# Three up-projections as seven half-size products each, and the last projection's first unit in another order

## The reference

```python
def hybrid_layer(x, mem, g_in, w_in, b_merge, g_mem, w_mem_kv, w_up_moba, w_up_dsa, w_up_cross, w_out):
    h = rmsnorm_2(x, g_in)
    z = h @ w_in          # split into (mq, mk, mv, mg, dq, dk, dv, dg, iq, ik, iw, xq, xg, glog)
    ...
    ya = moba_attention(mq, mk, heads(mv, MOBA_HEADS, HEAD_DIM)).reshape(B, S, MOBA_W)
    ya = (ya * jax.nn.silu(mg)) @ w_up_moba
    ...
    yb = (yb * jax.nn.silu(dg)) @ w_up_dsa
    ...
    yc = (yc * jax.nn.silu(xg)) @ w_up_cross
    gates = jax.nn.sigmoid(glog + b_merge).reshape(B, S, N_BRANCH_2, D_MODEL)
    u = gates[:, :, 0] * ya + gates[:, :, 1] * yb + gates[:, :, 2] * yc
    return x + u @ w_out
```

## Time and profile before

| what | value |
| --- | --- |
| median of 3 runs | 1574.53 us (1574.34 to 1576.32) |
| profiled execution, its own time | 1572.25 us |
| its span | 1570.5 us |
| mean granted TensorE clock over the span | 0.884 |
| from the end of `gl5` to the start of `w21` | 1494.80 to 1550.99 us |

### The profile page before, as it was taken

How to read it: one execution, slowest core, us unless ns; L and a number is a source line. 1 busy time by engine, 2 the same in 40 slices (tenths; PEclk the granted TensorE clock), 3 DMA queues, 4 the chain that set the end, 5 groups by cost and what they waited for, 6 DMA issues and landing times.

```text
span 1570.5 us, 21027 instructions
## 1 busy us (share of the span) xinstructions
PE 1257.4 (80%) x9222; PEld 818.6 (52%) x9222; DVE 562.7 (36%) x997; ACT 208.0 (13%) x426; POOL 2.8 (0%) x7
## 2 busy tenths in 40 slices
PE   9999999998666766665665665665666999999998
PEld 8989979974323312211221221221221588999986
DVE  5777467951001010010010010010010497798534
ACT  2003232020000000000000000000000211135401
POOL 0000000000000000000000000000000000000000
PEclk9999999999978977777777777787788999999999
DMA  9343274689999999999999999999999654434340
GB/s 374 143 162 139 85 264 170 271 362 433 443 428 433 437 431 433 434 434 436 434 432 434 436 434 432 434 437 434 431 431 430 275 214 161 161 109 170 112 153 36
DMA packets 20568, 506.61 MB, mean 323 GB/s; under 512 B 4240, under 2 KB 4368, under 8 KB 6544
## 3 DMA queue, kind: packets, MB, share of 16 engines
q1 hardware_dynamic: 20208, 505.28, 77.1%
q10 hardware_dynamic: 288, 0.26, 0.0%
HBM read 504.48 MB, written 1.05 MB: 322 GB/s over the span
## 4 chain that ended last, share of the span: by engine, by line
PE 54%; DMA 40%; DVE 4%; issue 1%; ACT 0%; SPq 0%; DVEq 0%; ACTq 0%
DMA ring<-in_experts 37%; PE psP L1400 13%; PE psP L779 10%; PE psP L1398 9%; PE psP L1347 8%; PE psP L827 4%; PE psA L842 2%; DMA arena<-in_experts 2%; DVE arena L2071 2%; PE psP L1440 2%; PE psB L1762 1%; PE psB L1333 1%; DVE ring L2071 1%; PE psA L758 1%; DMA X<-in_x 1%
## 5 line engine op out<-in xcount | busy, mean ns | idle before, releaser
L2071 DVE TENSOR_TENSOR X<-X,psA 128x512 f32<-128x512 f32 x66 | 45.2, 687 | 696.7 <-PE psA L842 682.5
L779 PE MATMUL psP<-ring,arena 128*32 128x512 f32 x1024 | 147.9, 730 | 127.8 <-DMA ring<-in_experts 127.8
L779 PE MATMUL psP<-arena 128*32 128x512 f32 x1024 | 145.3, 718 | 125.6 <-DMA arena<-in_experts 125.4
L779 PEld LDWEIGHTS psP<-ring,arena 128*32 128x32 f32 x1024 | 37.8, 131 | 234.4 <-issue 229.5
L779 PEld LDWEIGHTS psP<-arena 128*32 128x32 f32 x1024 | 35.0, 129 | 230.7 <-DMA arena<-in_experts 118.6
L1400 PE MATMUL psP<-arena,ring 128*128 128x128 f32 x992 | 116.9, 276 | 1.8 <-DVE score L2071 1.8
L1400 PEld LDWEIGHTS psP<-arena,ring 128*128 128x128 f32 x992 | 113.7, 192 | 3.0 <-issue 2.7
L827 PE MATMUL psP<-arena 128*32 128x512 f32 x512 | 73.8, 741 | 22.4 <-DMA arena<-in_experts 21.0
L827 PE MATMUL psP<-ring,arena 128*32 128x512 f32 x512 | 72.8, 726 | 23.3 <-DMA ring<-in_experts 21.9
L1400 PE MATMUL psP<-spare,ring 128*128 128x128 f32 x640 | 74.7, 275 | 0.0
L2071 DVE TENSOR_TENSOR ring<-ring 128x1024 f32<-128x1024 f32 x61 | 73.7, 1220 | 1.1 <-DMA ring<-in_u_dq 0.5
(11 more groups left out here) (354 smaller groups left out, 1429.7 us busy)
## 6 DMA issues: line engine op xcount, KB each, us to landing
arena<-in_experts SPq DMA_DIRECT2D x7, 4096.0 KB, 22.3
ring<-in_experts SPq DMA_DIRECT2D x7, 4096.0 KB, 23.3
ring<-in_u_gl SPq DMA_DIRECT2D x6, 2048.0 KB, 8.4
ring<-in_u_hq SPq DMA_DIRECT2D x2, 2048.0 KB, 22.6
ring<-in_u_hv SPq DMA_DIRECT2D x2, 2048.0 KB, 12.0
ring<-in_u_hg SPq DMA_DIRECT2D x2, 2048.0 KB, 8.6
ring<-in_u_ga SPq DMA_DIRECT2D x2, 2048.0 KB, 8.6
ring<-in_u_gb SPq DMA_DIRECT2D x2, 2048.0 KB, 9.0
```

Of the source, the lines that this page charges most:

```text
L779: mm = pe.matmul(z[j * CAP:(j + 1) * CAP, :], x[:, 4 * half + k, j * CAP:(j + 1) * CAP], held[c % 4][:, k // 2, j, (k % 2) * 512:(k % 2 + ...
L2071: return dve.tensor_tensor(o, a, b, op)
```

## The change

Each up-projection becomes seven products of half size in all three dimensions. `seven_up` issues them in two steps, four products and three, each product into a bank of its own (512 columns: 4 blocks of 128 outputs, 2 k, 128 tokens). Each step now uses both P0 and P1. `merge_up` adds up and gates each quarter at once. `halves` and `sums` get the three units; weight sums and half sums lie in areas of SBUF of their own. The end of the plan is written out anew, with sums and halves between the attention steps. `w20` gets an order of products of its own (`seven_final`), in which each product waits for the parts of the gated sum that it needs (`y_parts`), and `add_final` adds it up.

```diff
+OUT_PRODUCTS_2 = [(1, 0, 0), (2, 0, 256), (5, 0, 512), (6, 0, 768), (7, 1, 0), (3, 1, 256), (4, 1, 512)]
+UP_PRODUCTS = [[(2, 0, 0), (1, 0, 512), (6, 1, 0), (5, 1, 512)], [(7, 0, 0), (3, 0, 512), (4, 1, 0)]]
...
-    turn(9, 10, "gl5")
-    turn(10, None, "um0", "um1")
-    proj("ud0", "ud1")
-    sums("w20")
-    proj("ux0")
-    p.append(("halves_a", "z", ""))
-    proj("ux1")
+
+    p.append(("scores", 10, "A"))
+    sums("um")
+    p.extend([("halves", "um", ""), ("halves", "ud", ""), ("soft", 10, "")])
+    p.extend([("probsT", 9, "B"), ("normal", 10, ""), ("sums", ("ud", 0), "")])
+    p.extend([("head", ("gl5", 40), ""), ("pv", 9, "B")])
+    proj("gl5")
+    p.extend([("probsT", 10, "B"), ("sums", ("ud", 1), "")])
+    proj("um0")
+    p.append(("sums", ("ux", 0), ""))
+    proj("um1")
+    p.extend([("pv", 10, "B"), ("halves", "ux", ""), ("sums", ("ux", 1), "")])
+    proj("ud0")
+    p.append(("sums", ("w20", 0), ""))
+    proj("ud1")
+    p.append(("sums", ("w20", 1), ""))
+    proj("ux0", "ux1")
     p.append(("halves", "z", ""))
     proj("w20")
...
+            def seven_up(key, arg):
+
+                unit, step = arg[:2], int(arg[2])
+                regions, w, s = list(USE[key]), unit_ap(unit), h_sums[unit]
+                h = sg[{"m": "mg", "d": "dg", "x": "xg"}[unit[1]]]
+                t1, t2, t4 = sums_of(unit)
+                low, high = slice(0, 512), slice(512, 1024)
...
+                for n, half, at in UP_PRODUCTS[step]:
+                    (a, b), z = factors[n], ps[regions[half]]
+                    if n == 2:
+                        wait_empty(pe, ("pv", {"m": 8, "d": 5, "x": 10}[unit[1]]))
+                    if at == 0:
+                        may_fill(pe, key, regions[half])
+                    if n == 6:
+                        pe.wait_ge(halved, 4 * HALVES.index(unit) + 4)
+                        pe.wait_ge(summed, SUMMED[unit])
+                    if n == 4:
+                        pe.wait_ge(summed, SUMMED_LAST[unit])
+                    for o in range(4):
+                        for k in range(2):
+                            mm = pe.matmul(z[:, at + o * P:at + o * P + P], b[:, k, o * P:o * P + P], a[:, k, :],
+                                           start=(k == 0), stop=(k == 1))
...
+            def seven_final(key, arg):
...
+                for n, half, at in OUT_PRODUCTS_2:
+                    (a, b), z = factors[n], ps[regions[half]]
+                    if at == 0:
+                        may_fill(pe, key, regions[half])
+                    if n in (1, 2):
+
+                        pe.wait_ge(y_parts, {1: 1, 2: 3}[n])
+                    if n == 5:
+                        pe.wait_ge(summed, SUMMED_LAST[arg])
+                    if n in (5, 6, 7, 3):
+                        pe.wait_ge(halved, 4 * HALVES.index("z") + {5: 1, 6: 2, 7: 3, 3: 4}[n])
...
+            def merge_up(arg, key):
...
+                def gate(rows, t, n):
...
+                    y, x = gl[0][:, part, here], gl[g][:, part, here]
+                    if g == 0:
+                        i = tt(y, rows, y, ALU.mult)
+                    else:
+                        link(tt(x, rows, x, ALU.mult))
+                        i = tt(y, y, x, ALU.add)
+                    if g == 2:
+                        i.then_inc(y_parts, 1)
+
+                def block(z, kept_, region, t, n):
+
+                    rows = up_rows[n_gated[0] % 2]
+                    n_gated[0] += 1
+                    i = link(tt(rows, z, kept_, ALU.add))
+                    if region:
+                        dve.sem_inc(empty[region], 1)
+                    gate(rows, t, n)
+
+                if arg[2] == "0":
+                    dve.wait_ge(kept, q + 1)
+                    block(bank(r0, 0), p1, r0, 0, 0)
+                    wait_full(dve, key, r1)
+                    link(tt(u2, bank(r1, 0), p1, ALU.add))
+                    link(tt(w5, bank(r1, 512), u2, ALU.add))
+                    dve.sem_inc(empty[r1], 1)
+                else:
+                    dve.wait_ge(made, 2 * q + 2)
+                    block(bank(r0, 0), w5, None, 1, 1)
+                    tt(w7, bank(r0, 0), u2, ALU.add)
+                    wait_full(dve, key, r0)
+                    block(bank(r0, 512), w5, r0, 0, 1)
+                    dve.sem_inc(spent, 1)
+                    wait_full(dve, key, r1)
+                    block(bank(r1, 0), w7, r1, 1, 0)
```

More of the change, by code:

```diff
@@ L135 @@
 OUT = ("wo0", "wo1", "w20")
-FAST = FIRST + ["dq", "dv", "dk", "mv", "mq", "dg", "mk", "mg", "xq", "xg", "gl0", "gl1", "gl2", "gl3", "gl4", "gl5", "w20"]
+UP = ("um", "ud", "ux")
+FAST = FIRST + ["dq", "dv", "dk", "mv", "mq", "dg", "mk", "mg", "xq", "xg", "gl0", "gl1", "gl2", "gl3", "gl4", "gl5", "um", "ud", "ux", "w20"]
 BY_TOKENS = {*OUT, "hv0", "hv1", "cl", "hg0", "hg1", "dq", "dv", "dk", "mv", "mq", "mk"}
@@ L198, in proj @@
     def proj(*names):
-        p.extend(("proj", n, "PP" if n in FAST else "P") for n in names)
+        p.extend(("proj", n, "PP" if n in FAST or n[:2] in UP else "P") for n in names)
     def soft(g):
@@ new lines, in seven_final @@
+            def seven_final(key, arg):
+                regions, w = list(USE[key]), unit_ap(arg)
+                h, s = gl[0], h_sums["z"]
+                t1, t2, t4 = sums_of(arg)
+                low, high = slice(0, 256), slice(256, 512)
+                factors = {1: (h[:, 0:4, 0:P], w[:, 0:4, low]), 2: (h[:, 4:KC, 0:P], w[:, 4:KC, low]),
+                           3: (s[3], w[:, 4:KC, high]), 4: (h[:, 4:KC, P:S], t4),
+                           5: (s[0], t1), 6: (s[1], t2), 7: (s[2], w[:, 0:4, high])}
+                for n, half, at in OUT_PRODUCTS_2:
[8 more added lines that the diff above has]
+                        pe.wait_ge(halved, 4 * HALVES.index("z") + {5: 1, 6: 2, 7: 3, 3: 4}[n])
+                    for k in range(4):
+                        mm = pe.matmul(z[:, at:at + 256], a[:, k, :], b[:, k], start=(k == 0), stop=(k == 3))
+                    if n in (2, 3):
+                        mm.then_inc(made, 1)
+                    if n in (6, 4):
+                        mm.then_inc(full[regions[half]], 1)
@@ L1524, in _ @@
                     if arg == "w20":
-                        seven_out(key, arg, "z", ("proj", "ux0"), ("proj", "ux1"))
+                        seven_final(key, arg)
+                        continue
+                    if unit in UP:
+                        seven_up(key, arg)
                         continue
@@ L1601, in _ @@
                         token_major(key, arg, memT, w=wxva[:, 0], cols=P)
[L1602 to L1607, removed]
                     elif arg == "w21":
-                        wait_empty(pe, ("proj", "ux1"))
+                        pe.wait_ge(y_parts, 4)
                         if upto is None:
@@ L2124, in _ @@
             last_used |= {"wb0": "wa0", "wb1": "wa1"}
-            last_used |= {n: FAST[FAST.index(n) - 2] for n in FAST[len(FIRST) + 2:]}
+            last_used |= {n: FAST[FAST.index(n) - 2] for n in FAST[len(FIRST) + 2:FAST.index("um")]}
+            last_used |= {"um": "gl4", "ux": "gl5", "w20": "gl5"}
             def add_up(arg, part):
                 w, (t1, t2, t4) = unit_ap(arg), sums_of(arg)
-                low, high = slice(0, 256), slice(256, 512)
+                n = w.shape[2] // 2
+                low, high = slice(0, n), slice(n, 2 * n)
+                top, rest = slice(0, w.shape[1] // 2), slice(w.shape[1] // 2, w.shape[1])
                 if part == 0:
@@ L2371, in _ @@
                     r = region_of(key)
-                    if arg in OUT:
+                    if arg == "w20":
+                        add_final(arg, key)
+                    elif arg[:2] in UP:
+                        merge_up(arg, key)
+                    elif arg in OUT:
                         add_out(arg, key)
@@ L2449, in _ @@
                             signal_roped(rope(rows(ps[r]), 8, ropeA, ropeB, cos, sin, (r, USE[key][r])))
[L2450 to L2462, removed]
                 elif name == "level":
```

110 lines of the change are left out of this document (92 added, 18 removed).

## The result

The changed kernel takes 1579.28 us at the median of 10 executions (1576.88 to 1583.81), the kernel before 1573.66 (1571.31 to 1576.32): ratio 1.0039, 95% interval 1.0031 to 1.0046. It is slower by 5 to 7 us. The ten executions lie in two groups, five at 1576.88 to 1577.97 and five at 1580.58 to 1583.81. Its profiled execution has a span of 1575.7 us against 1570.5, 5.2 more, and an own time of 1577.48. Where `sums um` begins, near 1478 us, the two traces stand within 0.1 us of each other, and from the start of `w21` both need the same time (19.5 us), so all 5.2 lie between.

The account below looks back on a forecast made before the run. TensorE's work was taken to bound the stage, with VectorE's slack in question. Saving -3.9, wait +2.6, stalls +5.4, wake-ups +0.1 gave +4.2 us: execution 1576.4, median 1578.7, range 1574.3 to 1581.8.

Parts of the forecast that it names:

- the wait before `pv 9`: Sums and halves ahead of `soft 10` delay ScalarE's copy of `probsT 9`, which `pv 9` on TensorE needs: +2.6 us.
- VectorE's chain: VectorE's queue after `um0`: some 41 us of operations without a pause, where TensorE has 36 us of work.
- rival 1: TensorE's clock falls in the stall before `ux0`: 2.8 us lost there, some 2.2 passed on, 1580.9 us; 15%.
- three signs of being wrong: VectorE waits for TensorE between `um1` and `w20`; no pause before `pv 9`; or the clock row under 1.00.
- TensorE's saving, 3.9 us: Three up-projections at 112 instructions in 12.51 us each instead of 13.81: 3.9 us less TensorE work.
- The 4.4 from the formula: TensorE's saving estimated from the Trainium skill's matmul formula, 192 x 0.218 - 336 x 0.112, beside 3.9 from the rows.
- T: The end of `gl5`, the last gate product, on TensorE: 1494.80 us in the kernel before.
- Stalls behind T: TensorE waiting for VectorE after `gl5`, before `ud1`, `ux0`, `w20` and its third product: 5.4 us in all.
- Forecast stage: From the end of `gl5` until `w20` ends and its successor starts: 57.9 us forecast against 56.19 before.
- VectorE keeping pace: Dependent VectorE operations follow at 0.60 us, most stalls after `gl5` vanish: 1573.2 us, up to 1575.5; 15%.
- both covers holding: No waits before or after the end of `gl5`, the change gives just its 3.9 us: 1570.6 us; 6%.
- no wait before `pv 9`: `soft 10` comes earlier than added up, the chain after `gl5` stays: 1576.1 us; 6%.

Follow-up runs that it names:

- two units: Kernel before with only `um` and `ud` from seven products, `soft 10` ahead of their sums and halves, adds releasing their regions themselves: 1571.76 us, ratio 0.9990.
- the filler before `ux0`: Changed kernel plus 11 unused matmul calls on constants in TensorE's pause before `ux0`: 1578.12 us, ratio 1.0031.
- shorter sums: Changed kernel with `w20`'s four weight sums cut from 1024 to 32 elements, so most of its products use stale sums: 1574.86 us, ratio 1.0015.
- adds that release: Changed kernel with the adds releasing their PSUM region themselves instead of by a separate increment: 1577.15 us, ratio 1.0030.
- `soft 10` first: Changed kernel with `soft 10` moved ahead of the sums and halves of `um` and `ud`: 1575.52 us, ratio 1.0017.
- the changed kernel again: The changed kernel unaltered, run once more on the same chip as three other versions: 1579.59 us, ratio 1.0042 to the kernel before.
- the filler before `pv 9`: Changed kernel plus 7 unused matmul calls on constants in TensorE's pause before `pv 9`: 1578.81 us, ratio 1.0037.
- with the other: Changed kernel with 7 unused matmul calls before `pv 9` and 11 before `ux0`: 1578.07 us, ratio 1.0032.
- The two versions: Changed kernel with `soft 10` moved ahead, adds releasing regions, `w20`'s fourth sum late: ratio 1.0008; kernel before with only `um` and `ud` from seven products: 0.9990.
- `w20`'s new order alone: Kernel before with only `w20`'s products in the new order and its own adding up: 1574.37 us, ratio 1.0008.

## Why the prediction held

The forecast was +4.2 us and slower with 66%; the measured +5.6 on the medians (1579.28 - 1573.66) lies within its range, and the wait before `pv 9` and VectorE's chain are what the runs show. One term, the clock, was left out. The median that it named, 1578.7, came within 0.6 us of 1579.28 partly by luck: it was counted from 1574.53, and the kernel before measured 1573.66. Of its three signs of being wrong two appeared, both by the clock: the clock row fell under 1.00, and VectorE waited for TensorE behind `um1` (0.60 and 0.37 us).

- **TensorE's saving, 3.9 us.** Three times 112 instructions in 12.5 us, as priced. Right; with two units, 2.1 of 2.6 came out as time. (The 4.4 from the formula is worked out from unrounded times; with the 0.218 and 0.112 that stand beside it, it is 4.2.)
- **The wait before `pv 9`, +2.6.** T moved by 1497.24 - 1494.80 = 2.44. The sums took the 4.8 forecast, the eight halves 2.9 where 3.2 were put in. Undone by moving one step: shown.
- **Stalls behind T.** Forecast stage 57.9; with the clock held 58.03. Stall by stage, forecast and measured: before `ud1` 0.4 and 0.27, `ux0` 3.3 and 3.40, `w20` 0.7 and 0.72 (with the filler; 0.12 without), its third product 1.0 and 1.16. The price of a separate increment was too low (0.1; the rows say 0.2), and as the operations were otherwise a little cheaper the sum came out: two errors that cancelled. That VectorE's queue sets the time is shown from both sides: 3.6 us less by shorter sums, 1.28 by faster releases, and no pause once a third of the up-projections' additions is gone.
- **The clock: mis-sized.** The forecast left it at 1.00 and gave its fall in the pause before `ux0`, rival 1, 15% and 2.2 us, with 2.8 us lost on `ux0`. The fall is what happened: in the profiled execution and in the three others with that pause at 3.24 or 3.25 us (`soft 10` first, the changed kernel again, the filler before `pv 9`). It cost 1.5 us of `ux0` and 0.94 of the end where both are comparable. This is the term missing from the sum: 2.44 + (58.03 - 56.19) + 0.94 = 5.2, the whole difference of the spans. The chance was misread from the earlier trace rows: "2.99 us held, 4.38 did not" was taken as a line between them. The timeline of the kernel before shows 42 waits of TensorE of 2.74 us or more for the experts' weights. Behind 41 of them the next 32 instructions took 5.05 us or more, or the next 64 took 9.71 or more; the 2.99 is the one exception. Two of the others:

```profile
421.60 5.29 PE L827 MATMUL psP<-ring,arena 128*32 128x512 f32 x32 [2.74 <-DMA ring<-in_experts]
...
1176.74 10.03 PE L827 MATMUL psP<-arena 128*32 128x512 f32 x64 [3.34 <-DMA arena<-in_experts]
```

At full speed 32 such take 3.64 us and 64 take 7.07; the granted clock from 1176.74 to 1181 was 0.50. So a fall was what these rows led one to expect. The Trainium skill ("TensorE: Matmul & The Clock Gate", "Why this matters for your kernels") advises against pauses between bursts of matmuls. The trace agrees: 5.35 us for 32 instructions behind 3.24 us. Shorter pauses, 2.52, 2.12 and 1.73 to 1.75 us, were followed by a fall in some profiles too.
- **What the medians have beyond the spans.** Executions of the changed kernel spread over 7 us, of the kernel before over 5. Falls of the clock at three places, more or less deep, and up to 1.8 us from the experts' stage were seen in single profiles. How much each adds to the median is open: the fillers' ratios overlap with those without. The mean granted clock of each execution says that more is at work. In the 13 executions that have the filler before `ux0` (alone and with the other), the five with 0.894 or more took 1575.89 to 1578.07 us and the eight with 0.881 to 0.884 took 1577.48 to 1580.05. One fall to half for 3 us would lower that mean by 0.001 only (an estimate, 3 x 0.5 / 1576), so most of the difference in the mean comes from elsewhere in the run. In the kernel before the mean does not go with the time (medians 1572.81 above 0.89 and 1572.96 below, 23 executions). The cause is open.
- **Other rivals.** VectorE keeping pace, both covers holding, and no wait before `pv 9` are refuted by the profile after. The new order of `w20` was costed at nothing of its own. In the kernel before it costs 1.18 us; in the changed one its effect alone was not measured. The forecast also called `w21` edited nowhere, but it now waits for `y_parts`, not for `ux1`'s region to be released; its 19.5 us to the end are the same.

## What to carry to other kernels

A scheme with fewer products moves work from TensorE to the engine that adds them up: price both queues over the stretch where they run side by side, operation by operation, and convert only as many units as the adding engine can absorb. Here two of three paid, and with the third the gain of all was gone. The two versions also differ in `w20`'s order of products, and three units with the old order were not run, so how much of the 2.2 us between their stages (56.30 and 54.06) that order makes is not shown. Look in each in-order queue at what new work is put ahead of: the sums ahead of one softmax on VectorE held ScalarE, and through it TensorE. To price a pause of TensorE, look up every pause of its length in the trace and what followed, and not two.

## What the runs showed of the hardware

- A VectorE operation of 512 elements that waits for the one before it starts 0.71 us after it where the earlier one releases the region itself ("adds that release"), and 0.89 where a separate semaphore increment stands between (the changed kernel).
- Granted clock after pauses of TensorE, in this kernel and its versions:
  - 1.73 to 1.75 us before `probsT 6`: fell in 3 of 13 profiles (8 instructions in 1.60 to 1.66 us) and held in ten (1.06 or 1.07).
  - 2.11 or 2.12 us before `pv 9`: fell in one (16 in some 3.3 us) and held in four (some 1.9).
  - Before `ux0`: 2.52 us fell in one (5.44 for 32), 2.54 us held in another (3.81), 3.24 and 3.25 us fell in all four (5.35 to 6.55).
  - Waits for the experts' weights in the kernel before, 2.74 to 14.09 us: fell in 41 of 42. The longest after which it held in any profile was 3.46 us (`w20`'s new order alone, 32 instructions in 3.64).
- Extra products on constants in such a pause, put ahead of the wait, delay nothing where they end before it (`ux0` starts 3.40 us behind `ud1` with and without), and the clock was 1.00 behind them, in all three profiles with such a filler before `ux0`.
